# Loads of a neighbourhood bias moved ahead of the state-space tables, and its mask added by GpSimd after the second set of turns

## The chip, the cores and the metric

The kernel runs on 1 core of one Trainium2 chip. The metric is device time of one execution in microseconds (us). Before the change three runs took 2381.69, 2383.89 and 2387.66 us; the median is 2383.89 us. Engines are called by these names: PE is TensorE's matmul, PEld its weight load, DVE is VectorE, ACT is ScalarE, POOL is GpSimd, SP is SyncE; a q behind a name (ACTq) is the engine's instruction queue issuing a DMA.

## What is computed

Two transformer blocks on 256 tokens of width 2048, in float32. Only the first half of the first block touches the change. It projects the normalised input to queries, keys and values, to a state-space input u and to memory queries; three mixers work on them:

```python
h = rmsnorm(x, norm_mix_pre)
proj = h @ w_in
q_na, k_na, v_na, u_ssm, q_mem = jnp.split(proj, [...], axis=-1)
# neighbourhood attention: 8 heads of 128, each query sees a clamped window of a 4 x 64 grid
s = einsum(q, k_g) * scale + rpb_flat[:, bidx];  y_na = softmax(s) @ v_g
# state space (s5_mixer): 32 groups, 64 complex states, one direction forward, one backward
lam_bar = exp(lam * dt); h_t = lam_bar * h_(t-1) + b_bar @ u_t; y = Re(c @ h)
# memory cross attention: 4 heads against a normalised projection of mem
y = concat(rmsnorm(y_na), rmsnorm(y_ssm), rmsnorm(y_mem)) @ w_out; x = x + rmsnorm(y)
```

The neighbourhood attention runs in the kernel as dense 256 x 256 attention with a bias: relative-position values where a key lies in the window, plus a mask of -1e30 where its column lies outside.

## The kernel before

Everything is written out by hand: each engine has one program, in order, and they meet on semaphores. SP streams all weights through a ring of four 1 MB slots (`load`, L449) and waits only for a slot to be free. PE sets the order of the work: in the first block it does the memory projections (`group3`), then `group("u", xn)`, then the groups q0, k0, qm, q1, k1, v0, v1. A group is 16 k tiles of four matmuls (L564; one float32 matmul shows as two records); after each k tile it calls `steps()` (L1002), which weaves in the small products of the state space at fixed places: `bu(i)` (L773, eight matmuls on 32 rows, input of chunk i) and `ssm_y(i)` (L786, output of chunk i). By the tables at L535 to L540, bu(0) comes after the first k tile of q0, bu(1) after the ninth, y(0) after the 19th, bu(2) after the 22nd, and from there y(i) and bu(i+2) every 11 k tiles; y(6) and y(7) come after the 85th and 90th.

The state space is cut into 8 chunks (64 states by 8 groups, one tile of 128 x 1024 each). For each chunk
- POOL computes angles, the "turns" (L1736 to L1747, seven instructions). Chunk i begins when ACT has read the turns of chunk i-1 (L1735 waits for `turned_in`, L1483);
- ACT turns them into sine and cosine, `tables(i)` (L1482, L1483, L1485), when the turns are there and, from chunk 2 on, when DVE has finished chunk i-2;
- DVE rotates bu(i) by them (L2240 to L2248; its last read of the products is called "read"), scans twice (L2253, at L1758 and L2253 in the profile's lines), adds y(i-1) up (`yev`, L2223 or L1758) and rotates back ("h", L2258 to L2262). The decays that the scan needs come from ACT (L1490).

PE's bu(0) waits for two things of ACT: the copy of u out of PSUM (`evac("u")`, L1269) and the copy of the turned coefficients (`bbarT`, L1506). bu(1) waits for read(0), bu(i) for yev(i-2), y(i) for h(i) and read(i+1).

The bias: `na_loads()` (L1493) issues 17 DMAs from ACT's queue: the mask (L1495), and 16 loads of 128 KB (L1501), each of 64 partitions by 8 heads by 64 floats, so 512 runs of 256 bytes. They go to `na_bias`, which lies over `mem_low`, and to a half of `v1`. In the ACT program they stand behind the copy of k0. POOL's last instruction, behind the turns of all 8 chunks, waits for them (L1748) and adds the mask to the bias, 128 x 4096 (L1749). DVE needs the result at the first neighbourhood head (L1993), behind the four memory heads.

Of the kernel before, what the change touches and what calls it, by code (L numbers as in the profile page):

```python
# [7 lines left out]
P = 128  # L8
# [123 lines left out]
def program(nc, A, out, seen, book):  # L132
    f32 = mybir.dt.float32
    ALU = mybir.AluOpType
# [3 lines left out]
    with ctx:  # L138
        def sem(name):
            return ctx.enter_context(nc.semaphore(name))  # L140
# [23 lines left out]
        def tiles(t, a, n, w=S):  # L164
            return t[:, a:a + n * w].rearrange("p (t s) -> p t s", s=w)
# [26 lines left out]
        na_bias = tiles(xl_f, 0, 8, 512)  # L192
        na_mask = v1[:, 0, 512:1024]
# [65 lines left out]
        ssm_loaded, na_loaded = sem("ssm_loaded"), sem("na_loaded")  # L259
# [4 lines left out]
        def at(*name):  # L264

            return seen[name] if seen is not None else 1
# [278 lines left out]
        def _(pe):  # L545
# [364 lines left out]
            def duo_scores(p):  # L910

                x = duos[p]
                n = x["n"]
                for t, _, w in KEYS2:
                    w = min(w, n)
                    o = [ps[:, 4 + a, n * t:n * t + w] for a in range(2)]
                    for a in range(2):
                        last = nc.tensor.matmul(o[a], x["q"][a][:, P * t:P * t + P], x["k"][a][:, 0:w], start=True, stop=not x["extra"])
                    if x["extra"]:
                        rows = [slice(64 * a, 64 * a + 8) for a in range(2)]  # L920
                        col = [ident[64 * a:64 * a + 8, 64 * a + h:64 * a + h + 1] for a, h in enumerate(x["heads"])]
                        for a in range(2):
                            nc.tensor.matmul(o[a], fc8[rows[a], P * t:P * t + P], col[a].to_broadcast([8, w]), start=False, stop=False)
                        for a in range(2):
                            last = nc.tensor.matmul(o[a], col[a].to_broadcast([8, P]), fneg[rows[a], 0:w], start=False, stop=True)
                m.did(last, "scores2", p)
# [261 lines left out]
        def _(act):  # L1188
            m = Marks(act, act_done, book)
# [76 lines left out]
            def evac(name, dst, src=None, bias=None):  # L1266
                acc_done(name)
                src = acc4(name) if src is None else src
                nc.scalar.activation(dst, src, ACT.Copy).then_inc(acc_freed, 1)  # L1269

                act.wait_ge(acc_freed, ACC0[name] + (2 if name == "v1" else 1))
                m.own()
                m.did(nc.scalar.activation(st[:, 36:37], onec, ACT.Copy), "evac", name)
# [201 lines left out]
            def tables(i):  # L1475

                act.wait_ge(pool_done, at("turns", i))
                if i >= 2:
                    act.wait_ge(dve_done, at("h", i - 2))
                else:  # L1480
                    act.wait_ge(dve_done, at("bbar"))
                m.did(nc.scalar.activation(sinb[i % 2], turns, ACT.Sin, scale=6.283185))  # L1482
                m.did(nc.scalar.activation(cosb[i % 2], turns, ACT.Abs), "turned_in", i)  # L1483
                m.own()
                m.did(nc.scalar.activation(cosb[i % 2], cosb[i % 2], ACT.Sin, scale=-6.283185, bias=halfpi), "tables", i)  # L1485

            def decays(i):

                act.wait_ge(dve_done, at("scanned", i - 1))
                m.did(nc.scalar.activation(decay[:, :, 1:S], ssm[4][:, 4 * i:4 * i + 4].unsqueeze(2).to_broadcast([P, 4, S - 1]),  # L1490
                                           ACT.Copy), "decay", i)

            def na_loads():  # L1493

                act.dma_start(na_mask, A["na_mask"]).then_inc(na_loaded, 16)  # L1495
                rpb = A["na_rpb"]
                for r in range(S // GRID_W):
                    for rk in range(S // GRID_W):
                        src = bass.AP(rpb.tensor, (rk - r + WIN_H - 1) * RPB_W + WIN_W - 1, [[NA_HEADS * RPB_H * RPB_W - 1, GRID_W], [RPB_H * RPB_W, NA_HEADS], [1, GRID_W]])
                        c0 = S * (r // 2) + GRID_W * rk  # L1500
                        act.dma_start(na_bias[64 * (r % 2):64 * (r % 2) + 64, :, c0:c0 + GRID_W], src).then_inc(na_loaded, 16)  # L1501

            tables(0)
            evac("u", ut)
            act.wait_ge(pe_done, at("bbar_turned"))
# [5 lines left out]
            decays(2)  # L1511
            tables(3)
            evac("k0", k1[:, 0:4])
            na_loads()
            decays(3)
            tables(4)
            decays(4)
# [206 lines left out]
        @block.gpsimd  # L1724
        def _(pool):
            m = Marks(pool, pool_done, book)
            MAGIC = 12582912.0
            pool.wait_ge(dve_done, at("frac"))
            pool.wait_ge(ssm_loaded, 64)
            pool.wait_ge(split_used, SPLIT0["memv"] + 4)  # L1730
            time = iota.unsqueeze(1).to_broadcast([P, 4, S])
            for i in range(CHUNKS):
                col = lambda k: ssm[k][:, 4 * i:4 * i + 4].unsqueeze(2).to_broadcast([P, 4, S])
                if i:
                    pool.wait_ge(act_done, at("turned_in", i - 1))  # L1735
                m.did(nc.gpsimd.tensor_tensor(tmpb, time, col(8), ALU.mult))  # L1736
                m.own()
                m.did(nc.gpsimd.tensor_scalar(tmpb, tmpb, MAGIC, MAGIC, ALU.add, ALU.subtract))
                m.did(nc.gpsimd.tensor_tensor(turns, time, col(10), ALU.mult))
                m.own()  # L1740
                m.did(nc.gpsimd.tensor_tensor(turns, turns, tmpb, ALU.subtract))
                m.own()
                m.did(nc.gpsimd.tensor_tensor(tmpb, time, col(11), ALU.mult))
                m.own()
                m.did(nc.gpsimd.tensor_tensor(turns, turns, tmpb, ALU.add))
                m.own()
                m.did(nc.gpsimd.tensor_scalar(turns, turns, 0.5, -0.5, ALU.min, ALU.max), "turns", i)  # L1747
            pool.wait_ge(na_loaded, 16 * 17)  # L1748
            m.did(nc.gpsimd.tensor_tensor(na_bias, na_bias, na_mask.unsqueeze(1).to_broadcast([P, 8, 512]), ALU.add), "na_masked")  # L1749


        @block.vector
# [786 lines left out]
```

## Time and profile before

| | before |
|---|---|
| median of 3 runs | 2383.89 us |
| profiled execution | 2381.89 us, its span 2380.1 us |
| PE busy | 2300.5 us (97%) |
| DVE busy | 1370.6 us (58%) |
| ACT busy | 980.1 us (41%) |
| POOL busy | 166.7 us (7%), all of it in the first 264 us |
| mean granted TensorE clock | 0.987 |

The profile gives one row for an instruction or a run of like ones: its start and duration in us from the start of the span, the engine, the line, output and input tiles, and in brackets how long the engine was idle before it and who released it. The granted clock is a share of 2.4 GHz. The state space lies between 92 and 300 us; after it come attention (to about 385 us), the output product and the two large layers, then the second block.

### The profile page before, as it was taken

How to read it: one execution, taken by the hardware profiler on the slowest of the kernel's cores; microseconds unless marked ns; L12 is line 12 of the kernel's file. 1: busy time of each engine (PE TensorE's matmuls, PEld its weight loads, DVE VectorE, ACT ScalarE, POOL GpSimd, SP SyncE). 2: the span in 40 equal slices, each digit the busy share in tenths (PEclk: the TensorE clock that was granted, in tenths of full speed). 3: DMA queues.
4: the chain of work that ended last, by engine and by line, in shares of the span. 5: the costliest groups of instructions: out<-in, count | busy, mean ns of one | idle time of the engine just before them, and what ended most of it. 6: DMA issues, size and time to landing. Idle time of an engine off the chain costs nothing.

```text
span 2380.1 us, 31199 instructions
## 1 busy us (share of the span) xinstructions
PE 2300.5 (97%) x12622; PEld 1937.8 (81%) x12622; DVE 1370.6 (58%) x1483; ACT 980.1 (41%) x1290; POOL 166.7 (7%) x61
## 2 busy tenths in 40 slices
PE   7999999998999999999999999999999999999997
PEld 6887667787888888888888888787888888888886
DVE  5799846464554554444466478556545545444444
ACT  5212145343334344444444366535333444444443
POOL 0697400000000000000000000000000000000000
PEclk9999999999999999999999999999999999999999
DMA  8355334558656655565543533245566665555551
GB/s 304 114 141 142 114 100 166 177 132 223 193 181 189 183 187 195 193 245 192 190 146 115 198 107 93 100 153 164 174 192 188 192 191 181 194 194 194 194 194 71
DMA packets 151056, 404.24 MB, mean 170 GB/s; under 512 B 15168, under 2 KB 26688, under 8 KB 130368
## 3 DMA queue, kind: packets, MB, share of 16 engines
q1 hardware_dynamic: 135616, 385.51, 49.0%
q10 hardware_dynamic: 15360, 17.61, 3.4%
q8 instruction: 57, 0.93, 0.2%
q14 instruction: 23, 0.19, 0.0%
HBM read 396.80 MB, written 6.29 MB: 169 GB/s over the span
## 4 chain that ended last, share of the span: by engine, by line
PE 82%; DVE 8%; DMA 3%; ACT 3%; POOL 3%; issue 1%; ACTq 1%; SPq 0%; POOLq 0%; DVEq 0%
PE ps L657 18%; PE ps L695 11%; PE ps L697 11%; PE ps L696 11%; PE ps L658 9%; PE ps L564 4%; PE ps L580 2%; DVE w_low L1895 2%; DMA raw_weights<-in_w_ff 1%; PE ps L572 1%; DMA raw_weights<-in_w_mem_kv 1%; ACT w_high L1252 1%; PE ps L853 1%; PE ps L573 1%; PE ps L855 1%; PE ps L574 1%
## 5 line engine op out<-in xcount | busy, mean ns | idle before, releaser
L1895 DVE TENSOR_TENSOR w_low<-raw_weights,w_high 128x1024 fp32r<-128x1024 f32 (+1 forms) x628 | 738.4, 1218 | 801.8 <-ACT w_high L1252 801.7
L1252 ACT ACTIVATE w_high<-raw_weights 128x1024 fp32r<-128x1024 f32 (+1 forms) x628 | 628.7, 1049 | 846.9 <-PE ps L697 455.2
L657 PE MATMUL ps<-x_split,w_high 128*128 128x512 f32 x2048 | 724.1, 398 | 12.6 <-DVE w_low L1895 10.1
L658 PE MATMUL ps<-x_split,w_low 128*128 128x256 f32 x2048 | 576.5, 281 | 0.0
L657 PEld LDWEIGHTS ps<-x_split,w_high 128*128 128x128 f32 x2048 | 386.3, 189 | 105.8 <-DVE w_low L1895 10.3
L695 PE MATMUL ps<-w_high,x_split 128*128 128x512 f32 x1152 | 448.9, 390 | 3.1 <-DVE w_low L1895 3.1
L696 PE MATMUL ps<-w_low,x_split 128*128 128x512 f32 x1152 | 448.2, 389 | 0.0
L697 PE MATMUL ps<-w_high,x_split 128*128 128x512 f32 x1152 | 448.2, 389 | 0.0
L658 PEld LDWEIGHTS ps<-x_split,w_low 128*128 128x128 f32 x2048 | 389.2, 190 | 0.0
L695 PEld LDWEIGHTS ps<-w_high,x_split 128*128 128x128 f32 x1152 | 216.4, 188 | 48.8 <-DVE w_low L1895 4.0
L697 PEld LDWEIGHTS ps<-w_high,x_split 128*128 128x128 f32 x1152 | 216.3, 188 | 45.0
L696 PEld LDWEIGHTS ps<-w_low,x_split 128*128 128x128 f32 x1152 | 216.4, 188 | 44.8
L564 PE MATMUL ps<-x_over_high,raw_weights 128*128 128x256 f32 x768 | 173.2, 386 | 1.2 <-DVE x_over_high L1978 0.6
L564 PEld LDWEIGHTS ps<-x_over_high,raw_weights 128*128 128x128 f32 x768 | 146.9, 193 | 27.3 <-PE ps L773 3.9
L572 PE MATMUL ps<-x_split,w_high 128*128 128x256 f32 x416 | 122.4, 294 | 3.9 <-DVE w_low L1895 3.1
L573 PE MATMUL ps<-x_split,w_high 128*128 128x256 f32 x416 | 117.6, 283 | 0.0
L574 PE MATMUL ps<-x_split,w_low 128*128 128x256 f32 x416 | 117.5, 282 | 0.0
L572 PEld LDWEIGHTS ps<-x_split,w_high 128*128 128x128 f32 x416 | 79.4, 191 | 9.9 <-issue 4.5
L573 PEld LDWEIGHTS ps<-x_split,w_high 128*128 128x128 f32 x416 | 79.6, 191 | 0.1
L574 PEld LDWEIGHTS ps<-x_split,w_low 128*128 128x128 f32 x416 | 79.5, 191 | 0.0
L1279 ACT ACTIVATE region<-ps 128x1024 f32 (+1 forms) x32 | 32.8, 1025 | 108.9 <-PE ps L658 108.9
L580 PE MATMUL ps<-raw_weights,x_over_high 128*128 128x512 f32 x128 | 57.9, 594 | 0.0
(260 smaller groups left out, 2165.6 us busy)
## 6 DMA issues: line engine op xcount, KB each, us to landing
raw_weights<-in_w_ff SPq DMA_DIRECT2D x128, 1024.0 KB, 5.2
raw_weights<-in_w_up SPq DMA_DIRECT2D x64, 1024.0 KB, 5.2
raw_weights<-in_w_down SPq DMA_DIRECT2D x64, 1024.0 KB, 4.9
raw_weights<-in_w_in SPq DMA_DIRECT2D x62, 1024.0 KB, 5.6
raw_weights<-in_w_out SPq DMA_DIRECT2D x32, 1024.0 KB, 4.9
raw_weights<-in_w_mem_kv SPq DMA_DIRECT2D x8, 1024.0 KB, 15.4
t_table<-region ACTq DMA_DIRECT2D x1, 4096.0 KB, 45.8
region<-t_table ACTq DMA_DIRECT2D x1, 3072.0 KB, 17.8
```

The source lines that it names most:

```text
L564: last = nc.tensor.matmul(acc[:, c], w[:, P * c:P * c + P], x, start=(kt == 0 and c % 2 == 0), stop=(kt == kts - 1), skip_group_check=True)
L572: nc.tensor.matmul(o, h, xh_, start=(first and c % 2 == 0), stop=False, skip_group_check=True)
L573: nc.tensor.matmul(o, h, xl_, start=False, stop=False, skip_group_check=True)
L574: last = nc.tensor.matmul(o, wl[:, P * c:P * c + P], xh_, start=False, stop=done, skip_group_check=True)
L580: last = nc.tensor.matmul(acc[:, t, 0:n], x[:, P * t:P * t + P], w, start=(kt == 0), stop=(kt == kts - 1))
L657: nc.tensor.matmul(o, wh[:, q, w], xs[:, kt], start=(kt == 0), stop=False, skip_group_check=True)
L658: last = nc.tensor.matmul(o[:, 0:S], wl[:, q, w], xh[:, kt], start=False, stop=(kt == KT - 1), skip_group_check=True)
L695: nc.tensor.matmul(o, h, wh[:, r], start=(first and j == 0), stop=False, skip_group_check=True)
L696: nc.tensor.matmul(o, h, wl[:, r], start=False, stop=False, skip_group_check=True)
L697: last = nc.tensor.matmul(o, l, wh[:, r], start=False, stop=True, skip_group_check=True)
L1252: nc.scalar.activation(split_slot(wh_t, k)[:, r], ring_slot(n)[:, r], ACT.Copy).then_inc(rounded, 1)
L1895: V.tensor_tensor(split_slot(wl_t, k)[:, r], ring_slot(n)[:, r], split_slot(wh_t, k)[:, r].bitcast(f32), ALU.subtract).then_inc(split_read ...
```

## The change

`na_loads()` moves from behind the third group's copy to a place before everything of the state-space tables, behind the copy of the memory values. The mask add and its wait move from behind the loop over 8 chunks into it, behind the turns of chunk 1.

```diff
+            na_loads()
             tables(0)
             evac("u", ut)
             act.wait_ge(pe_done, at("bbar_turned"))
@@
             tables(3)
             evac("k0", k1[:, 0:4])
-            na_loads()
             decays(3)
@@
                 m.did(nc.gpsimd.tensor_scalar(turns, turns, 0.5, -0.5, ALU.min, ALU.max), "turns", i)
-            pool.wait_ge(na_loaded, 16 * 17)
-            m.did(nc.gpsimd.tensor_tensor(na_bias, na_bias, na_mask.unsqueeze(1).to_broadcast([P, 8, 512]), ALU.add), "na_masked")
+                if i == 1:
+                    pool.wait_ge(na_loaded, 16 * 17)
+                    m.did(nc.gpsimd.tensor_tensor(na_bias, na_bias, na_mask.unsqueeze(1).to_broadcast([P, 8, 512]), ALU.add), "na_masked")
```

## Rows read from the trace of the kernel before

**Rows 1.** The page, first part: busy time of each engine.
```profile
PE 2300.5 (97%) x12622; PEld 1937.8 (81%) x12622; DVE 1370.6 (58%) x1483; ACT 980.1 (41%) x1290; POOL 166.7 (7%) x61
```
**Rows 2.** Waits of PE, 60 to 440 us: total us, times, longest.
```profile
PE ps L773 <- DVE mixed L1758: 3.0, 1, 3.0
...
PE ps L773 <- DVE mixed L2223: 0.7, 1, 0.7
```
**Rows 3.** Timeline of ACT, 94 to 102 us: start, duration, instruction, idle before.
```profile
94.15 1.04 ACT L1482 ACTIVATE region<-mixed 128x1024 f32<-128x1024 f32 x1
...
97.76 1.03 ACT L1269 ACTIVATE region<-ps 128x1024 f32<-128x1024 f32 x1 [0.44 <-PE ps L564]
...
99.50 1.88 ACT L1506 ACTIVATE region<-ps 128x2048 f32<-128x2048 f32 x1 [0.49 <-PE ps L998]
```
**Rows 4.** Timeline of ACT's queue at the loads.
```profile
168.15 0.33 ACTq L1495 DMA_DIRECT2D region<-in_na_mask  x1
168.52 16.67 ACTq L1501 DMA_DIRECT2D x_over_low<-in_na_rpb  x16
```
**Rows 5.** Line L1501's instructions: durations in ns, landing in us.
```profile
L1501 ACTq DMA_DIRECT2D x_over_low<-in_na_rpb x16: 657/716/4301, 168.5 to 184.5; - x16
...
DMA to landing us min/median/max: 5.0/6.0/8.8
```
**Rows 6.** Timeline of PE at the woven products (idle before, in brackets).
```profile
101.44 2.36 PE L773 MATMUL ps<-region 32*128 32x256 f32 x16 [0.24 <-ACT region L1506]
...
137.78 0.64 PE L786 MATMUL ps<-mixed,region 128*32 128x256 f32 x8
...
145.02 2.36 PE L773 MATMUL ps<-region 32*128 32x256 f32 x16
...
193.16 2.36 PE L773 MATMUL ps<-region 32*128 32x256 f32 x16 [0.70 <-DVE mixed L2223]
...
269.00 2.38 PE L773 MATMUL ps<-region 32*128 32x256 f32 x16 [3.02 <-DVE mixed L1758]
```
**Rows 7.** Timeline of DVE: start, duration, instruction, idle before.
```profile
103.85 1.23 DVE L1758 TENSOR_TENSOR mixed<-ps,region 128x1024 f32<-128x1024 f32 x1 [9.80 <-PE ps L773]
...
111.60 2.00 DVE L1758 TENSOR_TENSOR scratch<-mixed,scratch 128x1024 f32<-128x1024 f32 x1
113.63 6.12 DVE L2253 TENSOR_TENSOR_SCAN scratch<-mixed,scratch 128x1024 f32<-128x1024 f32 x2
...
132.21 2.36 DVE L1758 TENSOR_TENSOR scratch<-ps,region 128x1024 f32<-128x1024 f32 x2
...
136.63 6.12 DVE L2253 TENSOR_TENSOR_SCAN scratch<-mixed,scratch 128x1024 f32<-128x1024 f32 x2
142.87 0.48 DVE L2223 SCALAR_TENSOR_TENSOR mixed<-region,gains,ps 128x256 f32<-128x256 f32 x1
...
186.39 6.13 DVE L2253 TENSOR_TENSOR_SCAN scratch<-mixed,scratch 128x1024 f32<-128x1024 f32 x2 [3.81 <-ACT mixed L1490]
...
255.37 13.04 DVE L2253 TENSOR_TENSOR_SCAN scratch<-mixed,scratch 128x1024 f32<-128x1024 f32 x2
...
281.12 4.47 DVE L2253 TENSOR_TENSOR_SCAN scratch<-mixed,scratch 128x1024 f32<-128x1024 f32 x2
```
**Rows 8.** Timeline of POOL: end of the turns of chunk 1, next chunk, the mask add.
```profile
111.48 1.04 POOL L1747 TENSOR_SCALAR mixed<-mixed 128x1024 f32<-128x1024 f32 x1
114.64 2.97 POOL L1736 TENSOR_TENSOR scratch<-region,rinv 128x1024 f32<-128x1024 f32 x1 [2.12 <-ACT region L1483]
...
254.23 9.85 POOL L1749 TENSOR_TENSOR x_over_low<-x_over_low,region 128x4096 f32<-128x4096 f32 x1
```
**Rows 9.** Windows: length, busy time by engine, granted clock (after POOL), DMA share, GB/s.
```profile
196.00:199.40 3.40, 3.40 (x10) 2.74 (x9) 3.40 (x2) 0.00 (x0) 3.32 (x2) 0.52 0.31 121
...
271.00:274.40 3.40, 3.33 (x11) 2.42 (x8) 3.28 (x4) 0.00 (x0) 0.00 (x0) 0.53 0.00 0
```
**Rows 10.** ACT's issues at the start of the kernel.
```profile
3.96 0.45 ACTq L1428 DMA_DIRECT2D residual<-in_xT  x1
```

## The prediction

> **What bounds the kernel now.** I read the page first: PE is busy 97% of the span [rows 1], so the sum is made on PE's line of work. Whatever delays PE early delays the end, and only PE's idle time can be won. Then the waits of PE in the stretch that the change touches: from 60 to 440 us it waits 3.0 us and 0.7 us at L773 (the state-space products bu) for DVE [rows 2], and other waits there aren't tied to the bias. So the most that moving the bias can remove is 3.7 us of waits and what follows them. Third, the timelines of ACT, POOL and DVE side by side, to see how far each woven product is from being late: the reader is to see which engine arrives last at bu and y.
>
> Both waits are the doing of the bias. The loads hold ACT's queue for 17.04 us (168.15 to the last issue's end at 185.19, the mask's among them) [rows 4]; DVE's fourth pair of scans then waits 3.81 us for the decays [rows 7], and PE is 0.70 us late at bu(4) [rows 6]. The mask add takes POOL 9.85 us from 254.23 [rows 8], and beside it DVE's two scans take 13.04 us, against 6.12 beside the ordinary turns and 4.47 with POOL silent [rows 7]. They end 4.3 us after the add, just what a pair takes alone, so the add holds the scans off until it ends. That makes bu(7) 3.02 us late [rows 6]. Both waits are followed by a clock step: 0.52 and 0.53 granted in 3.4 us behind each [rows 9], that is near 1.2 of 2.4 GHz, and half of 3.4 us is lost each time, 1.7 us.
>
> **Part 1, what goes.** The two waits, 0.70 + 3.02 = 3.7 us, and two clock steps, 2 x 1.7 = 3.4 us, if PE arrives after DVE in the new order (worked out below: it does). Together -7.1 us. The floor of this gain is 3.7 us, since the step may come back for other reasons.
>
> **Part 2, the loads ahead of tables(0).** In the new place ACT issues 17 DMAs from 94.1 us on. Queued behind them on ACT are tables(0), the copy of u and the copy bbarT [rows 3]. PE's bu(0) waits for both copies; it stands behind the first k tile of q0, and today it starts 0.24 us after PE is free, released by that copy [rows 6]. So there is no cover: PE runs dry at once. ACT's own idle time before the copies, 0.44 + 0.49 us [rows 3], is used up first. Stall added to PE: 17.04 - 0.93 = 16.1 us. DVE stands still with it, since it idles until bu(0) today already (9.80 us) [rows 7]. Bounds of the issue time: with 17 issues near the median of 0.716 us and 0.03 between them it is 12.3 us, so 11.4 us of stall; the difference is mostly one long issue of 4.30 us [rows 5]. SP's weight loads share the DMA engines at both places, so I keep 17.04, the nearest row, and allow a second long issue at the upper end: 3.6 more, 19.7 us. While PE stands the ring fills and SP stops, so no weights will be late.
>
> PE then has been idle for 16 us. Waits of 0.70 and 3.02 us were enough for the clock step here [rows 9], so I expect bu(0) at the lower level: 2.36 us of matmuls [rows 6] become twice that, +2.4 us for PE and DVE alike. Bounds: 1.7 us as in the rows, 4.1 us if the low clock also lasts for another such step behind bu(0). Sum so far 18.5 us, from where PE, DVE and nearly POOL (it waits for tables(0), +17.0) move together. Times below are those of before, to be read with this shift.
>
> **Part 3, the mask add behind turns(1).** Its wait costs nothing: the last load lands at most 8.8 us after its issue [rows 5], near 94.1 + 17.0 + 8.8 = 120 us, while the turns of chunk 1 end at 112.5 + 17 = 129.5 us [rows 8]. Queued behind the add on POOL are the turns of chunks 2 to 7. Today POOL idles 2.12 us there for ACT [rows 8], so turns(2) come 9.85 - 2.1 = 7.7 us later. POOL has a lead: turns(1) are done at 112.5, the scans of chunk 1 begin at 136.6 [rows 7], 24.1 us later, of which some 3 us go to the tables and 10 us to DVE's six rotations (103.85 to 113.6 in chunk 0) [rows 7]. The 11 us left are more than 7.7, so late turns alone cost nothing. The cost is on DVE: at 112.5 us it is at a subtraction of two SBUF tiles and then the two scans [rows 7], the same neighbours that stood beside the add at 254. Lower bound of DVE's delay d: the measured 13.04 - 6.12 = 6.9 us. Upper: the whole 9.85 plus the contention with turns(2), which now follow at once, about 11 us. I take 8.7, the add's 9.85 less the 1.1 us in which DVE's subtraction (2.00 us, 1.2 alone) ran first, as nearer to the rows.
>
> What PE feels of d: y(0) needs read(1), which ends at 134.6 [rows 7], and PE is there at 137.8 [rows 6]: 3.2 us of cover, so it waits d - 3.2. bu(2) needs yev(0), ready at 143.35 [rows 7], and PE is there at 145.0 [rows 6]: 1.7 us of cover. The larger demand counts, since the first wait is contained in the second: d - 1.7 = 7.0 us. A clock step in the k tiles between y(0) and bu(2) is absorbed by the same wait. From there DVE's period is 23.0 us (scans at 113.63 and at 136.63) [rows 7], PE's 23.7 (from bu(2) to bu(4), less the 0.70, halved) [rows 6], so PE gains no further wait. At bu(4) PE comes 7.0 us later than now, DVE 8.7 - 3.8 = 4.9: no wait. At bu(7) DVE has shed 6.9 us more: no wait. That is why part 1 counts in full. The cover for d at bu(2) is 1.7 us; without it 1.7 more would be due.
>
> **The sum.** 16.1 + 2.4 + 7.0 - 7.1 = +18.4 us. The profiled execution took 2381.89 us (span 2380.1 and 1.8 around it), which would become 2400.3. It lies 2.0 us under the median of the runs; on the median 2383.89 the forecast is 2402.3 us.
>
> **A rule that speaks for the change.** In the rows the 17 issues follow each other on ACT's queue without a break and nothing else runs there [rows 4]. The Trainium skill, page "DMA: Bandwidth & Descriptors", section "Rules for kernel authors", advises to issue a DMA early, compute, and wait for its semaphore late, so that the fixed setup overlaps. By that rule parts 2 and 3's wait would be free and the sum would keep only the mask's effect and the gain. The trace differs: the setup is overlapped only for engines that don't stand behind the issuing queue, and here PE stands behind it.
>
> **Rivals.**
> (a) The mask is free for DVE: POOL's add falls into another phase, DVE's first-read operations come from PSUM and aren't held up, and y(0) and bu(2) keep their cover. For it: four of DVE's six operations ahead of the scans read PSUM. Against it: the same neighbours at 254 us. It gives 16.1 + 2.4 - 7.1 = +11.4 us, 2395.3. Chance 0.14.
> (b) Not slower: the issues are cheap at the new place. At the start of the kernel an issue of large runs takes ACT 0.45 us [rows 10]; 17 x 0.45 and small gaps are 8.1 us, less 0.93 is 7.2 us of stall; with no clock step and the mask free the sum is 7.2 - 7.1 = +0.1 us, 2384.0. It decides in the change's favour once an issue costs under 0.45 us and DVE isn't held. Against it: all 16 issues took at least 0.657 us [rows 5], with 256-byte runs on a queue that was empty. The same case holds if the rule above were right. Chance 0.04.
> (c) Heavier: POOL, without its 2.12 us of rest and one add behind, and DVE get in each other's way at every chunk; DVE's period grows from 23.0 to about 25, past PE's 23.7, and PE waits at each later bu. Six chunks of 1.3 us and a clock step at two or three of them: +12 us, sum +30, 2414. For it: DVE has no idle time in the loop, so each hold is felt. Against it: turns and chunks keep their order. Chance 0.09.
>
> **How the numbers follow.** Forecast 0.73, (a) 0.14, (b) 0.04, (c) 0.09. Its own bounds: low 11.4 + 1.7 + 5.2 - 7.1 = +11.2, high 19.7 + 4.1 + 9.3 - 3.7 = +29.4; both ends at once are unlikely. The range takes in (a) and the upper bound and leaves out (b) and most of (c): 2393 to 2413. About 0.3%, 7 us, is what a measurement of this kernel can tell from no change. The forecast, (a) and (c) lie above it; (b) splits between same and faster: slower 0.95, same 0.03, faster 0.02.
>
> **What would show it.** In the changed profile: PE idle some 16 us before the first L773, released by L1506; the ACT queue's 17 issues at 94 to 111 us, with one long one; a low granted clock behind the gap; the first pair of scans at 12 to 16 us, or the subtraction ahead of them near 10; PE waiting 4 to 6 us at the first L786 and little at the third L773; no waits at the fifth and eighth; scans of chunk 6 at about 6 us. The prediction is wrong if the issues take under 10 us, if PE isn't idle at bu(0), if DVE's first scans stay at 6 us, or if waits appear at later products.

## The result, and the profile after

| | before | after |
|---|---|---|
| median of 4 runs | 2382.79 us | 2398.59 us |
| profiled execution | 2381.89 us, span 2380.1 | 2397.38 us, span 2395.6 |
| PE busy | 2300.5 us (97%) | 2303.3 us (96%) |
| mean granted TensorE clock | 0.987 | 0.985 |

The ratio is 1.0069, with a 95% interval of 1.0053 to 1.0086: the changed kernel is slower by 12.6 to 20.5 us. The forecast was 2402.3 us and the range 2393 to 2413. On the profiled pair the change costs 15.5 us of span; 14.9 of them are there at the last of the woven products (the last record of L786 starts at 299.2 before and at 314.1 after), so the rest of the kernel hardly matters. In the changed kernel some lines have a number one higher than before: L1507 is the copy bbarT, L1750 the mask add, L2254 the scan. The experiments' kernels shift them by a few lines too (by up to four upwards or downwards), so rows are best told apart by engine, tiles and time.

The waits of PE between 60 and 460 us, in total, how often, the longest. They answer [rows 2]: the two old waits (3.0 and 0.7 us for DVE at L773) are gone, and two others are there, at L773 for ACT and at L786. That at L853 (2.8 us) was there before, too.

```profile
PE ps L773 <- ACT region L1507: 14.2, 1, 14.2
PE ps L853 <- DVE w_low L1896: 2.8, 2, 1.8
PE ps L786 <- DVE scratch L1759: 2.5, 1, 2.5
```

The timeline of ACT and its queue. It answers [rows 3, 4]: start, duration, instruction, idle before.

```profile
93.88 0.33 ACTq L1495 DMA_DIRECT2D region<-in_na_mask  x1
94.24 14.74 ACTq L1501 DMA_DIRECT2D x_over_low<-in_na_rpb  x16
109.09 1.06 ACT L1482 ACTIVATE region<-mixed 128x1024 f32<-128x1024 f32 x1 [15.02 <-issue]
...
113.32 1.86 ACT L1507 ACTIVATE region<-ps 128x2048 f32<-128x2048 f32 x1
```

So tables(0), both copies and all that waits for them stand behind 15.1 us of issues. The timeline of PE at the woven products answers [rows 6]:

```profile
115.23 4.24 PE L773 MATMUL ps<-region 32*128 32x256 f32 x16 [14.19 <-ACT region L1507]
...
135.74 2.36 PE L773 MATMUL ps<-region 32*128 32x256 f32 x16
...
158.18 1.08 PE L786 MATMUL ps<-mixed,region 128*32 128x256 f32 x8 [2.47 <-DVE scratch L1759]
...
167.06 2.36 PE L773 MATMUL ps<-region 32*128 32x256 f32 x16
...
214.43 2.36 PE L773 MATMUL ps<-region 32*128 32x256 f32 x16
...
285.50 2.36 PE L773 MATMUL ps<-region 32*128 32x256 f32 x16
```

Read against [rows 6], these are the same products later by 13.8 us (bu(0)), 20.4 (y(0)), 22.0 (bu(2)), 21.3 (bu(4)) and 16.5 (bu(7)). bu(1) comes 17.9 us later than its 117.88 of before. So PE loses 22 us in the first three chunks and wins back 7 in the last four. Windows of the changed kernel (length, busy time by engine, granted clock, DMA share, GB/s) show what the clock does, to set beside [rows 9]:

```profile
103.00:115.20 12.20, 0.00 (x0) 0.00 (x0) 0.00 (x0) 6.03 (x6) 3.94 (x2) 0.52 0.78 120
115.20:119.50 4.30, 4.16 (x16) 2.39 (x16) 0.00 (x0) 0.00 (x0) 4.22 (x3) 0.50 0.00 0
119.50:123.40 3.90, 3.85 (x9) 3.13 (x10) 3.84 (x3) 0.00 (x0) 3.74 (x3) 0.50 0.00 0
123.50:128.00 4.50, 4.50 (x21) 3.89 (x20) 4.43 (x4) 0.50 (x1) 4.41 (x3) 0.94 0.00 0
157.70:161.10 3.40, 2.92 (x28) 1.57 (x32) 3.33 (x3) 2.05 (x3) 1.20 (x2) 0.56 0.00 0
```

The clock falls to its lower level, 1.2 of 2.4 GHz, while PE is idle, and stays there for 8.2 us of work behind the gap; it falls once more at y(0). The scans of DVE and the mask add of POOL answer [rows 7, 8]:

```profile
128.58 14.66 DVE L2254 TENSOR_TENSOR_SCAN scratch<-mixed,scratch 128x1024 f32<-128x1024 f32 x2
160.09 6.12 DVE L2254 TENSOR_TENSOR_SCAN scratch<-mixed,scratch 128x1024 f32<-128x1024 f32 x2
...
127.43 9.82 POOL L1750 TENSOR_TENSOR x_over_low<-x_over_low,region 128x4096 f32<-128x4096 f32 x1
137.20 3.89 POOL L1736 TENSOR_TENSOR scratch<-region,rinv 128x1024 f32<-128x1024 f32 x1
```

The add takes what it took before (9.82 us), but now it stands at the scans of chunk 0 (14.66 us) and no longer at those of chunk 6, which take 4.47.

### The profile page after: what moved, and what is told of

Its sections match the earlier page's. It is cut to its first block, busy times and chain, and to the rows that moved or that the text cites. A ratio compares the mean times of both kernels' runs of the same rounds, so it can differ in the third digit from the quotient of the medians.

```text
span 2395.6 us, 31199 instructions
## 1 busy us (share of the span) xinstructions
PE 2303.3 (96%) x12622; PEld 1936.3 (81%) x12622; DVE 1369.8 (57%) x1483; ACT 979.8 (41%) x1290; POOL 168.4 (7%) x61
## 4 chain that ended last, share of the span: by engine, by line
PE 82%; DVE 7%; ACT 2%; DMA 2%; issue 1%; ACTq 0%; DVEq 0%; SPq 0%
PE ps L657 19%; PE ps L695 11%; PE ps L696 11%; PE ps L697 11%; PE ps L658 9%; PE ps L564 5%; PE ps L580 2%; DVE w_low L1896 2%; DMA raw_weights<-in_w_ff 1%; PE ps L572 1%; PE ps L853 1%; PE ps L855 1%; PE ps L854 1%; ACT w_high L1252 1%; PE ps L754 1%; PE ps L573 1%
## 5 line engine op out<-in xcount | busy, mean ns | idle before, releaser
L657 PE MATMUL ps<-x_split,w_high 128*128 128x512 f32 x2048 | 725.5, 399 | 12.3 <-DVE w_low L1896 9.8
L657 PEld LDWEIGHTS ps<-x_split,w_high 128*128 128x128 f32 x2048 | 387.4, 189 | 108.2 <-DVE w_low L1896 9.8
```

Source lines behind the costliest of these rows:

```text
L657: nc.tensor.matmul(o, wh[:, q, w], xs[:, kt], start=(kt == 0), stop=False, skip_group_check=True)
```

## Experiments

Two theories were to be told apart at first. The first puts the loss on ACT's queue: PE stands behind the issues. The rival puts it on the mask add or on the traffic of the loads. Then each part was undone or shrunk by itself. A table of all runs; "last product" is the start of the last record of L786 against 299.2 us before. It leaves out the rest of the kernel, where executions of one and the same kernel differ by several us. "Turns 5" are the turns of chunk 5.

| kernel | ratio, 95% interval | span, us | last product |
|---|---|---|---|
| the change | 1.0069, 1.0053 to 1.0086 | 2395.6 | +14.9 |
| loads moved, add last | 1.0079, 1.0051 to 1.0108 | 2393.2 | +18.8 |
| add behind turns 5, loads not moved | 1.0015, 0.9992 to 1.0038 | 2383.6 | +5.5 |
| loads behind the copy, add last | 0.9984, 0.9968 to 1.0000 | 2371.2 | -5.3 |
| the same, add by head from chunk 2 on | 0.9977, 0.9959 to 0.9994 | 2372.6 | -6.7 |
| the change, add by head | 1.0040, 1.0022 to 1.0058 | 2387.8 | +11.3 |
| the change, one load | 0.9999, 0.9984 to 1.0015 | 2377.2 | -1.5 |
| the change, PE kept busy | 1.0056, 1.0031 to 1.0080 | 2395.6 | +13.9 |
| loads behind the copy, whole add behind turns 1 | 0.9997, 0.9977 to 1.0017 | 2381.1 | +0.7 |
| loads behind the copy, add by head at the end | 0.9974, 0.9961 to 0.9987 | 2370.3 | -7.3 |
| the same again | 0.9952, 0.9936 to 0.9968 | 2365.7 | -7.3 |
| one load first, add by head at the end | 0.9961, 0.9946 to 0.9976 | 2378.6 | -7.6 |

**Loads alone.** The loads as in the change, the mask add where it was.

```diff
+            na_loads()
             tables(0)
@@
-            na_loads()
             decays(3)
```

> Only the loads are moved ahead of the tables; the mask add stays behind the last turns. Theory (queue order on ScalarE makes the stall): TensorE idles about 14 us before its first L773 and runs bu(0) and some 4 us behind it at the low clock, and since VectorE no longer waits 3.8 us for the decays, the waits at bu(4) and bu(7) go too although the mask add has not moved: 14.2 + 1.9 + 2.1 - 7.1 = about +11 us on the kernel before, ratio 1.0046. Rival (the mask add, or its wait for the loads, carries the loss): under +5 us. Rival (the old wait at bu(7) is the mask add's alone): the 3.0 us wait stays, +15 to +16 us.

Measured: the stall is there (15.1 us at bu(0), 4.24 us for bu(0)), so it belongs to the loads. But the expected +11 us is missed: the last product comes 18.8 us later. The second rival was nearer in this: the add's wait doesn't go, it moves and grows. PE doesn't wait at bu(7) but at y(5). Timelines of PE, POOL and DVE of this kernel:

```profile
280.36 3.64 PE L786 MATMUL ps<-scratch,region 128*32 128x256 f32 x32 [5.95 <-DVE scratch L1758]
...
266.91 9.83 POOL L1749 TENSOR_TENSOR x_over_low<-x_over_low,region 128x4096 f32<-128x4096 f32 x1
...
270.50 7.33 DVE L1758 TENSOR_TENSOR scratch<-mixed,scratch 128x1024 f32<-128x1024 f32 x1
```

The add now meets a subtraction that stands between DVE's reads of bu(6), not the scans behind them, so it delays read(6) and with it y(5). DVE had slipped before that: its scans of chunks 3, 4 and 5 start at 198.44, 223.23 and 250.56, 24.8 and 27.3 us apart instead of 23.0. The slip begins at 205.28, where yev(2) waits 0.72 us for PE's y(2), so PE's lateness comes back to DVE, which then meets POOL's turns at other places: the two operations at 208.19 take 6.09 us, against 4.06 for the same pair in the kernel before. That this shift causes the longer distances is read from the order in time; no run isolates it. Beside this kernel the mask's move is a gain of 3.9 us (18.8 to 14.9), not a cost.

**Mask add alone.** Behind the turns of chunk 5, loads in their old place.

```diff
+                if i == 5:
+                    pool.wait_ge(na_loaded, 16 * 17)
+                    m.did(nc.gpsimd.tensor_tensor(na_bias, ...), "na_masked")
-            pool.wait_ge(na_loaded, 16 * 17)
-            m.did(nc.gpsimd.tensor_tensor(na_bias, ...), "na_masked")
```

> Only the mask add is moved, from behind the last turns to behind the turns of chunk 5 (behind chunk 1 it would deadlock with the loads in their old place). Theory (the add holds VectorE's scans about 8.5 us wherever it stands, and TensorE has some 3 us of cover): scans of chunk 4 take about 14.7 us, TensorE waits about 4 us at y(4) and 1 to 2 us at bu(6), nothing at bu(7): between 0 and +3 us on the kernel before. Rival (an earlier mask add falls into GpSimd's idle time and is free): no new waits, 3.0 us and a clock step gone, -4.7 us.

```profile
209.09 14.68 DVE L2254 TENSOR_TENSOR_SCAN scratch<-mixed,scratch 128x1024 f32<-128x1024 f32 x2
...
224.42 4.24 PE L773 MATMUL ps<-region 32*128 32x256 f32 x16 [7.80 <-DVE mixed L2224]
```

The scans (DVE, first row) take the expected 14.7 us, against the rival that an early add is free. The expectation had the place of PE's wait wrong, and its size: behind scans i stands yev(i-1), and bu(i+1) waits for it, so the add at scans 4 hits bu(5) at once, 7.80 us, and the clock is low behind it until about 233 us (bu takes 4.24 us). The last product comes 5.5 us later, outside the expected 0 to 3. Behind the scans of chunk 0 there is no yev, which would explain why the change's own place costs PE less (4.1 us, below); no run tests this alone.

**Loads behind the copy.** One place later in ACT's program than PE's release.

```diff
             m.did(nc.scalar.activation(bbarT..., ACT.Copy), "bbarT")
+            na_loads()
             tables(1)
@@
-            na_loads()
             decays(3)
```

> The loads are issued behind the copy of the turned coefficients (L1506) and ahead of tables(1), one place later than TensorE's release; the mask add stays last. Theory (queue order, not the traffic): no idle time before bu(0); issues take about 15 us from 101.4 us on, in a stretch where ScalarE waits 11 us for GpSimd anyway; tables(1) come 4 us late and VectorE still needs them later; the wait at bu(4) goes, that at bu(7) shrinks to about 1.6 us: -4 to -5.5 us on the kernel before. Rival (the DMA traffic or any early issue costs TensorE time by itself): 5 us or more slower than before.

```profile
99.99 15.89 ACTq L1501 DMA_DIRECT2D x_over_low<-in_na_rpb  x16
...
101.55 2.36 PE L773 MATMUL ps<-region 32*128 32x256 f32 x16 [0.24 <-ACT region L1506]
...
265.30 2.36 PE L773 MATMUL ps<-region 32*128 32x256 f32 x16 [1.68 <-DVE mixed L1758]
```

Held: the issues are as long (15.89 us, ACT's queue, first row), but there is no idle time at bu(0) except the old 0.24 us, no wait at bu(4), 1.68 us at bu(7) (PE, the other rows), and the last product comes 5.3 us earlier. So the traffic of the loads in nearly the same stretch costs PE nothing that shows. The clock did not fall behind the 1.68 us (granted 1.00 up to 276 us).

**The same, mask add by head.** Eight adds of 128x512 between the turns. The diff shows what differs from the kernel above.

```diff
-            pool.wait_ge(na_loaded, 16 * 17)
-            m.did(nc.gpsimd.tensor_tensor(na_bias, ...), "na_masked")
+                if i == 2:
+                    pool.wait_ge(na_loaded, 16 * 17)
+                for h in {2: (0, 1), 3: (2,), 4: (3,), 5: (4,), 6: (5,), 7: (6, 7)}.get(i, ()):
+                    m.did(nc.gpsimd.tensor_tensor(na_bias[:, h], na_bias[:, h], na_mask, ALU.add), "na_masked")
```

> As the kernel before it, and the mask add cut by head into 8 adds of 128x512, one or two of them behind the turns of each chunk from 2 to 7. Theory (the cost of the add is its length, 9.8 us in which VectorE's scans are held; a piece of about 1.2 us fits into the 2.1 us in which GpSimd waits for ScalarE): scans stay at 6 to 7.5 us, no waits of TensorE at the woven products, both clock steps gone: -7 us on the kernel before, ratio 0.997. Rival (every piece holds the scans by its own length, 8.5 us in all, as the whole add does): waits stay at late products, -2 us to +2 us.

Held in size (-6.7 us), and scans stay at 6.23 us. But the pieces aren't free: one takes 3.25 us on POOL, not the expected 1.2; DVE's scans are 23.93 us apart, slower than PE's 23.7, and PE waits 0.18 us twice. Over more chunks this might add up; no run shows it.

**The change, mask add by head.** Pieces behind the turns of chunks 1 to 7.

```diff
-                    m.did(nc.gpsimd.tensor_tensor(na_bias, ...), "na_masked")
+                for h in {1: (0,), 2: (1,), ..., 6: (5,), 7: (6, 7)}.get(i, ()):
+                    m.did(nc.gpsimd.tensor_tensor(na_bias[:, h], na_bias[:, h], na_mask, ALU.add), "na_masked")
```

> The changed kernel with its mask add cut by head: 8 adds of 128x512, one behind the turns of each chunk from 1 to 6 and two behind the last. Theory (the stall behind the load issues is the loss, the whole add costs some 4 us more): idle time of 14 us and the low clock behind it stay, the first pair of scans takes 6 to 7 us instead of 14.7, the wait at y(0) and the clock step behind it go: +11 us on the kernel before, 4 to 5 us less than the changed kernel. Rival (pieces hold VectorE as long as the whole): no gain on the changed kernel, +15 us.

```profile
115.29 4.25 PE L773 MATMUL ps<-region 32*128 32x256 f32 x16 [14.33 <-ACT region L1507]
...
128.64 7.09 DVE L2255 TENSOR_TENSOR_SCAN scratch<-mixed,scratch 128x1024 f32<-128x1024 f32 x2
```

Held: +11.3 us at the last product, with the stall (first row, PE) and without the long scans (second row, DVE) or the wait at y(0). So of the change's 14.9 us, 3.6 are due to the add in one piece, and 11.3 are the loads' stall and its low clock less the old waits.

**The change, one load.** The bias comes in the order of its tile; the host only gathers. The bytes are the same.

```diff
-                for r in range(S // GRID_W):
-                    for rk in range(S // GRID_W):
...
-                        act.dma_start(na_bias[64 * (r % 2):64 * (r % 2) + 64, :, c0:c0 + GRID_W], src)...
+                act.dma_start(na_bias.rearrange("p h c -> p (h c)"), A["na_pre"]).then_inc(na_loaded, 16)
```

> The changed kernel, but the bias is laid out by the host in the order of its tile (a gather, no arithmetic), so 16 loads of 256-byte runs become one load of 16 KB rows, in the same place ahead of tables(0); the bytes are the same. Theory (the stall is ScalarE's time to issue, one long row of small runs that the queue takes no faster than it drains): issues under 1.5 us, TensorE idle under 1.5 us at bu(0), clock stays up; what is left is the whole mask add at chunk 0: waits of about 5 us at y(0) and up to 2 us at bu(2), less 7.1 us: -1 to +2 us on the kernel before. Rival (moving 2 MB there costs by its traffic or its landing): 10 us or more slower than before.

```profile
94.15 0.45 ACTq L1496 DMA_DIRECT2D x_over_low<-in_na_pre  x1
...
101.16 2.36 PE L773 MATMUL ps<-region 32*128 32x256 f32 x16 [0.24 <-ACT region L1502]
...
141.79 1.08 PE L786 MATMUL ps<-mixed,region 128*32 128x256 f32 x8 [4.22 <-DVE scratch L1754]
```

Held, at the good end (-1.5 us at the last product). The issue takes 0.45 us (first row, ACT's queue) instead of 14.74, and PE isn't late at bu(0). The only new wait is the mask add's at y(0), 4.22 us with the low clock in the product. The early place isn't harmful; 16 issues of 512 small runs ahead of PE's release are. This run changes the number of issues and the length of the runs together: sixteen issues of 0.45 us would be 7.2 us, an estimate, so about half of the 14.74 us may go with the number.

**The change, PE kept busy in the gap.** PE repeats the first k tile of q0 eight times; each repeat starts the sum anew.

```diff
+                if k == 0:
+                    for _ in range(8):
+                        wide(acc4("q0"), ring_slot(SLOT0["q0"])[:, 0:512], xn[:, 0], KT, 0)
```

> The changed kernel, and TensorE repeats the first k tile of q0 eight times (same result: each repeat starts the sum anew) where it otherwise stands idle for 14 us, so that only the clock is different behind the stall. Theory (low clock behind the stall costs 1.9 us on VectorE's chain through bu(0), and 2.1 us more on TensorE alone, which the wait at y(0) gives back): bu(0) takes 2.4 us instead of 4.2, the wait at y(0) grows to about 4.6 us, and the kernel is 2 us faster than the changed one. Rival (the 4.0 us of low clock count in full): 4 us faster. Rival (the clock has no part in it): same.

```profile
116.53 2.35 PE L773 MATMUL ps<-region 32*128 32x256 f32 x16 [1.60 <-ACT region L1510]
...
157.49 0.64 PE L786 MATMUL ps<-mixed,region 128*32 128x256 f32 x8 [2.86 <-DVE scratch L1762]
...
166.11 2.36 PE L773 MATMUL ps<-region 32*128 32x256 f32 x16 [1.31 <-DVE mixed L2227]
```

Windows of this kernel at bu(0) and behind it, as in the result:

```profile
116.50:118.80 2.30, 2.19 (x16) 1.41 (x16) 0.00 (x0) 0.00 (x0) 2.30 (x2) 1.00 0.00 0
118.80:122.20 3.40, 3.32 (x10) 2.61 (x9) 3.22 (x3) 0.00 (x0) 3.32 (x2) 0.54 0.00 0
```

bu(0) takes 2.35 us instead of 4.24, so the clock's part is real. The issues took 15.95 us in this run against 14.74, so bu(0) starts 1.3 us later than in the change, and still the third bu starts 0.95 us earlier: 2.2 us won on equal issues, near the 2 expected and short of the full 4. The gap wasn't filled to its end, and behind the 1.60 us that were left of it the clock fell for 3.4 us from 118.8 on (the windows above, granted 1.00 and then 0.54). So on equal issues 2.4 us are won up to bu(1), not 4; y(0), at the full clock now, wins 1.6 more. Of these 4.0 us 1.7 went back into waits: 2.86 us at y(0) and 1.31 at bu(2), against 2.47 in all in the change. In time the two kernels can't be told apart (1.0056 and 1.0069, the intervals overlap).

**Loads behind the copy, whole add behind the turns of chunk 1.**

```diff
+            na_loads()
             tables(1)
@@
-            na_loads()
             decays(3)
@@
+                if i == 1:
+                    pool.wait_ge(na_loaded, 16 * 17)
+                    m.did(nc.gpsimd.tensor_tensor(na_bias, ...), "na_masked")
-            pool.wait_ge(na_loaded, 16 * 17)
-            m.did(nc.gpsimd.tensor_tensor(na_bias, ...), "na_masked")
```

> Loads behind the copy, the whole mask add behind the turns of chunk 1 as in the changed kernel. Now GpSimd reaches the add before the last load has landed. Theory: the issues end near 115.5 us and land by 124 us, so GpSimd waits some 8 to 10 us from about 114 us on and begins the turns of chunk 2 at about 133 us instead of 114.6; VectorE's lead is used up and TensorE waits 3 to 6 us at y(0), y(1) or bu(3): -2 to +4 us on the kernel before. Rival (the landing is in time): like the whole add behind chunk 1 with one load, -1 to -3 us.

```profile
122.62 8.89 POOL L1750 TENSOR_TENSOR x_over_low<-x_over_low,region 128x4096 f32<-128x4096 f32 x1 [10.19 <-DMA x_over_low<-in_na_rpb]
131.47 2.88 POOL L1736 TENSOR_TENSOR scratch<-region,rinv 128x1024 f32<-128x1024 f32 x1
...
172.48 3.00 PE L773 MATMUL ps<-region 32*128 32x256 f32 x16 [2.71 <-DVE mixed L2224]
```

Held. POOL (first two rows) waits 10.19 us for the landing and begins the turns of chunk 2 at 131.5 us; PE pays 1.0 us at y(1), 2.7 at bu(3) and 0.7 at bu(5), and all that the later loads won is gone. Here the wait for the loads, which moved with the add, matters; in the change the stall gave the loads time to land, and POOL began the add without a wait (127.43 us).

**Loads behind the copy, add by head at the end.** Measured twice.

```diff
+            na_loads()
             tables(1)
@@
-            na_loads()
             decays(3)
@@
             pool.wait_ge(na_loaded, 16 * 17)
-            m.did(nc.gpsimd.tensor_tensor(na_bias, ...), "na_masked")
+            for h in range(8):
+                m.did(nc.gpsimd.tensor_tensor(na_bias[:, h], na_bias[:, h], na_mask, ALU.add), "na_masked")
```

> Loads behind the copy of the turned coefficients, as in the third experiment, and the mask add by head, all eight adds behind the last turns, where the kernel before has its whole add. Theory (one long add holds a scan for its whole length, short ones let VectorE in between them): the scans of chunk 6 take 5 to 8 us instead of 13, the wait of 1.7 us at bu(7) goes, and unlike with pieces between the turns GpSimd's loop isn't longer: -7 to -9 us on the kernel before, ratio 0.9965. Rival (GpSimd takes the next add before VectorE gets in): scans of 13 us, as in the third experiment.

> The version of the tenth label once more (loads behind the copy of the turned coefficients, eight adds by head behind the last turns), in more rounds: -7 us on the kernel before, ratio 0.997, and an interval that leaves out 1. If the first result was chance: 0.999 or above.

```profile
250.28 18.74 POOL L1750 TENSOR_TENSOR x_over_low<-x_over_low,region 128x512 f32<-128x512 f32 x8
...
251.43 6.46 DVE L2254 TENSOR_TENSOR_SCAN scratch<-mixed,scratch 128x1024 f32<-128x1024 f32 x2
...
263.31 2.36 PE L773 MATMUL ps<-region 32*128 32x256 f32 x16
```

Held. The eight adds take POOL 18.74 us (first row) instead of 9.85, which nobody waits for, and the scans of chunk 6 beside them 6.46 us instead of 13.04; bu(7) starts without a wait, 5.7 us earlier. The last product comes 7.3 us earlier, what the prediction's first part put at 7.1 (two waits and two clock steps). In both runs the version is faster than the kernel before with an interval below 1: 0.9974 and 0.9952. So it beats both kernels, the one before by up to half a per cent.

**One load first, add by head at the end.** The 16 loads and the add behind turns 1 are gone, as above.

```diff
+                act.dma_start(na_bias.rearrange("p h c -> p (h c)"), A["na_pre"]).then_inc(na_loaded, 16)
@@
+            for h in range(8):
+                m.did(nc.gpsimd.tensor_tensor(na_bias[:, h], na_bias[:, h], na_mask, ALU.add), "na_masked")
```

> One load from a bias laid out by the host, ahead of tables(0) as in the changed kernel, and eight adds by head behind the last turns. Theory (the changed place is harmful only by the length of the issues, the add only by its length): no waits of TensorE at any woven product, same as the version beside it, -7 us, ratio 0.997. Rival (the early place has a cost of its own): slower than the version beside it by 3 us or more.

Held: -7.6 us at the last product, no wait at a woven product but the old 0.24 us, and a time (0.9961) that can't be told from the version beside it (0.9952, overlapping intervals). The profiled execution has a span of 2378.6 us all the same, 12.9 more than the 2365.7 of that version. They come little by little in products that were not changed, as the first and last records of one line show in this kernel and in that version's second run:

```profile
L695 PE MATMUL ps<-w_high,x_split x1152: 389/389/988, 855.3 to 2353.4; 128*128 128x512 f32 x192
```

```profile
L695 PE MATMUL ps<-w_high,x_split x1152: 387/389/592, 847.2 to 2340.5; 128*128 128x512 f32 x192
```

This kernel is 8.1 us behind at the first of them and 12.9 at the last. No wait of PE is longer by more than 0.6 us: PE is busy 2305.8 us in this execution and 2291.7 in the other, with the same matmuls (those of L657 have a median of 398 and 392 ns), at a granted clock of 0.989 and 0.990. Why the matmuls take longer stays open; the comparison rests on the timed runs.

## Why the prediction was right, point by point

**What goes.** Right to within 0.1 us. From bu(2) to the last product PE wins back 22.0 - 14.9 = 7.1 us, the two waits and two clock steps of -7.1.

**The loads' stall.** The mechanism was right: 14.19 us of idle time released by the copy. The size was 16.1 us in the sum and is 14.0 (less the old 0.24). The term that was off is the issue time: 15.1 us instead of 17.04. The long issue came back, as supposed, but took 3.2 us rather than 4.3, and the median issue 0.657 rather than 0.716 us. The second long issue of the upper bound didn't come.

**The clock behind it.** Put at 2.4 us, and it was 4.1, the upper bound. bu(0) took 4.24 us instead of 2.36 (+1.9), and from its end to bu(1) PE took 16.3 us instead of 14.1 (+2.2), for the low clock outlasted bu(0) by 4 us.

**The mask add on DVE.** Put at 8.7 us; the scans took 14.66 - 6.12 = 8.5 us more.

**What PE feels of it.** Here the sum was most off: 7.0 us forecast, 4.1 measured (22.0 at bu(2) less 17.9 at bu(1)), as 2.5 us of wait and 1.6 us of low clock in y(0). The sentence that failed is that PE and DVE move together from bu(0) on. The 2.2 us of slow k tiles are PE's alone, so PE came later to y(0) and the cover was 3.2 + 2.2 us rather than 3.2; and DVE's first subtraction took 2.20 instead of 2.93 us, so DVE was 7.8 us late instead of 8.7. Less 5.4 that is 2.4 us of wait at y(0), not the 4 to 6 that the prediction gave as a sign. Nor was the second demand the larger one: bu(2) had no wait, since y(0)'s wait and slow product had already made PE late enough. I had noted that a clock step between y(0) and bu(2) would be absorbed, and not asked the same of one ahead of y(0). The experiment with PE kept busy shows the exchange: of the 4.0 us of low clock that it takes away, 1.7 come back as waits.

**The sum.** 14.0 + 4.1 + 4.1 - 7.1 = 15.1 us on the trace, against 18.4 (the last product is 14.9 later, since PE came to the stall 0.2 us earlier than before). Terms were too high by 2.1 and 2.9 us and one too low by 1.7, so that the sum came within 3.3 us is in part luck: the errors partly cancel. The mechanisms themselves, the stall, the low clock, the held scans and the two waits gone, are those of the forecast.

**The rivals.** (a), the mask free, is refuted in the change (14.66 us); its time, +11.4, is near that of the kernel with the add cut by head (+11.3), where the add costs PE no wait; in that sum, too, the stall's excess and the clock's shortfall nearly cancel. (b), cheap issues, is refuted for small runs, and its price of 0.45 us is what one load of large rows took. (c), DVE and POOL in each other's way at every chunk, isn't seen in the change (scans 23.0 us apart from chunk 1 to 6), but it is real: with the loads alone moved the distance grew to 24.8 and 27.3 us. With the loads behind the copy and the whole add behind turns 1, where POOL came late with the turns, three of the distances were 25.2 to 26.5 us. It had a chance of 0.09 and might have had more.

**The rule on early issue.** That a DMA issued early overlaps its setup, which the Trainium skill advises on the page "DMA: Bandwidth & Descriptors", section "Rules for kernel authors", holds here once nothing that PE waits for stands behind the issuing queue: one place further down the same 17 issues cost nothing, and the last product comes 5.3 us earlier than before. In the change, where PE stood behind them, they cost 14.0 us.

## What to carry to other kernels

Before moving DMA issues up, list what stands behind them on the issuing queue, and which engine has no cover for it; 16 issues of small runs were 15 us of that engine. Behind the last instruction that another engine is about to need, the same issues were free. A long side task on GpSimd next to a loop of VectorE was paid for by its length as long as it was one piece; cut it up, and put the pieces where nobody waits for GpSimd any more.

## What the runs showed of the hardware that I had not expected

- The cost of issuing doesn't follow the bytes: 2 MB as 16 loads of 512 runs of 256 bytes took ACT's queue 14.7 to 16.8 us, the same 2 MB as one load of 16 KB rows 0.45 us. How much of this is the number of loads and how much the short runs, no run here separates. In each kernel with 16 loads one of the issues was far longer than the rest, 2.7 to 4.3 us, for a reason that stays open.
- After 14 us of idle time the clock stayed at the lower level for 8.2 us of PE's work (115.2 to 123.4 us), longer than the 3.4 us behind the short waits [rows 9]; behind the 7.80 us of the kernel with the add behind turns 5 it stayed for about 9 us. A short wait didn't always bring it down: 0.70 us did in the kernel before and 1.60 us in the kernel with PE kept busy, but 1.68 us with the loads behind the copy did not, nor did 2.86 us at y(0) with PE kept busy.
- The same pair of scans beside the same turns of POOL took 5.19 us in some kernels and 6.12 in others, with 22.9 or 23.0 us between chunks; the two engines' instructions fall beside each other differently there, which looks like the cause but was not tested, and in one kernel a wait of 0.72 us was followed by gaps of 24.8 and 27.3 us.
- Eight adds of 128x512 take POOL 18.74 us beside DVE's work, one of 128x4096 9.85 us. A piece takes 1.27 to 3.26 us, and the scans beside them 6.46 us instead of 13.04: cut up, it is the add that is held for part of the time.
